# Seven block products instead of eight for two of the three input projections of a short-convolution mixer

## The reference, cut to what matters

```
h    = rms_norm(x) * gain                    # 256 x 2048
b, c, u = h @ W_in split in three            # W_in: 2048 x 6144
y    = W_out( b * causal_conv3(c * u) )      # depthwise, 3 taps, W_out: 2048 x 2048
x    = x + y
```

## Time and profile before

| | us |
|---|---|
| median of 3 runs | 2103.23 (2100.74 to 2107.02) |
| the profiled execution, device time | 2106.77 |
| its span in the trace | 2105.0 |
| PE busy | 2075.5 (99%) |
| PE weight loads busy | 1728.1 (82%) |
| VectorE busy | 1358.3 (65%) |
| ScalarE busy | 1099.4 (52%) |
| GpSimd busy | 556.6 (26%) |
| mean transfer rate | 187 GB/s |

### The profile page before, as it was taken

How to read it: one execution, slowest core, us unless ns; L and a number is a source line. 1 busy time by engine, 2 the same in 40 slices (tenths; PEclk the granted TensorE clock), 3 DMA queues, 4 the chain that set the end, 5 groups by cost and what they waited for, 6 DMA issues and landing times.

```text
span 2105.0 us, 24328 instructions
## 1 busy us (share of the span) xinstructions
PE 2075.5 (99%) x9634; PEld 1728.1 (82%) x9634; DVE 1358.3 (65%) x1378; ACT 1099.4 (52%) x1260; POOL 556.6 (26%) x292
## 2 busy tenths in 40 slices
PE   9998999999999999999999999999999999999999
PEld 8888777888888888888888888888888888888887
DVE  5787868954888358873442333478738994389832
ACT  6677555644555445554544444555545554455542
POOL 3676630023000420004454444310040003400033
PEclk9999999999999999999999999999999999999999
DMA  7533355556555565645566565556466555655554
GB/s 251 161 120 120 131 178 192 180 169 230 180 202 180 193 206 193 236 159 181 180 199 191 183 187 190 171 201 243 155 213 219 177 183 190 236 184 188 188 190 161
DMA packets 208577, 394.29 MB, mean 187 GB/s; under 512 B 11472, under 2 KB 22096, under 8 KB 208464
## 3 DMA queue, kind: packets, MB, share of 16 engines
q1 hardware_dynamic: 207888, 392.21, 55.7%
q10 hardware_dynamic: 576, 0.53, 0.1%
HBM read 390.60 MB, written 2.10 MB: 187 GB/s over the span
## 4 chain that ended last, share of the span: by engine, by line
PE 90%; issue 3%; DVE 3%; ACT 2%; POOL 1%; DMA 0%; SPq 0%; DVEq 0%; ACTq 0%; POOLq 0%
PE pair L654 14%; PE pair L656 14%; PE pair L655 14%; PE pair L731 9%; PE pair L729 9%; PE pair L730 9%; PE pair L714 5%; PE pair L715 5%; PE pair L716 5%; PE tbank L744 2%; DVE w_lo L1595 1%; DVE pair L1748 1%; POOL cv L620 1%; ACT w_hi L1161 1%; DVE s_raw L1990 0%
## 5 line engine op out<-in xcount | busy, mean ns | idle before, releaser
L1161 ACT ACTIVATE w_hi<-w_raw 128x1024 fp32r<-128x1024 f32 x608 | 642.3, 1059 | 653.5 <-PE pair L656 418.9
L608 POOL TENSOR_TENSOR w_lo<-w_raw,w_hi 128x1024 fp32r<-128x1024 f32 x191 | 472.3, 2473 | 1533.1 <-ACT w_hi L1161 1533.1
L1595 DVE TENSOR_TENSOR w_lo<-w_raw,w_hi 128x1024 fp32r<-128x1024 f32 x417 | 537.6, 1290 | 490.8 <-ACT w_hi L1161 490.6
L729 PE MATMUL pair<-w_hi,xT_hi 128*128 128x512 f32 x880 | 342.4, 389 | 0.4 <-DVE w_lo L1595 0.4
L731 PE MATMUL pair<-w_hi,xT_lo 128*128 128x512 f32 x880 | 342.4, 389 | 0.0
L730 PE MATMUL pair<-w_lo,xT_hi 128*128 128x512 f32 x880 | 342.3, 389 | 0.0
L1161 ACT ACTIVATE w_hi<-s_raw 128x1536 fp32r<-128x1536 f32 x154 | 229.2, 1488 | 160.0 <-PE pair L731 119.1
L1595 DVE TENSOR_TENSOR w_lo<-s_raw,w_hi 128x1536 fp32r<-128x1536 f32 x154 | 269.7, 1761 | 59.5 <-ACT w_hi L1161 59.2
L654 PE MATMUL pair<-w_hi,yT_hi 128*128 128x512 f32 x704 | 274.7, 390 | 0.0
L656 PE MATMUL pair<-w_hi,yT_lo 128*128 128x512 f32 x704 | 274.0, 389 | 0.0
L655 PE MATMUL pair<-w_lo,yT_hi 128*128 128x512 f32 x704 | 273.9, 389 | 0.0
(11 more groups left out here) (187 smaller groups left out, 2659.7 us busy)
## 6 DMA issues: line engine op xcount, KB each, us to landing
w_raw<-in_w_down SPq DMA_DIRECT2D x176, 512.0 KB, 4.2
w_raw<-in_w_up SPq DMA_DIRECT2D x110, 512.0 KB, 6.5
w_raw<-in_w_gate SPq DMA_DIRECT2D x110, 512.0 KB, 3.6
w_raw<-in_sc_in SPq DMA_DIRECT2D x96, 512.0 KB, 3.9
s_raw<-in_w_gate SPq DMA_DIRECT2D x44, 768.0 KB, 8.6
s_raw<-in_w_up SPq DMA_DIRECT2D x44, 768.0 KB, 8.2
w_raw<-in_w_in SPq DMA_DIRECT2D x52, 512.0 KB, 4.0
w_raw<-in_w_out SPq DMA_DIRECT2D x32, 512.0 KB, 3.5
```

What stands on the lines that cost most here:

```text
L608: nc.gpsimd.tensor_tensor(w_lo[at], raw(o), w_hi[at].bitcast(F32), ALU.subtract).then_inc(w_lo_pool, 1)
L729: nc.tensor.matmul(b, x_hi(k, t), w_hi[:, r, kk, :], start=(first[t] and kk == 0), stop=False)
L1161: nc.scalar.activation(w_hi[:, o % RING, tiles_of(o), :], raw(o), ACT.Copy).then_inc(w_hi_ready, 1)
L1595: nc.vector.tensor_tensor(w_lo[at], raw(o), w_hi[at].bitcast(F32), ALU.subtract).then_inc(w_lo_dve, 1)
```

## The change

The projections c and u (`cg` and `cu`) run as one unit `("sc", j)` of 17 slots, in the manner of the FFN's units, followed by a plain `bg` job of 8 slots, which moves to PSUM pair 1. So a block has 25 slots, and the block products leave out one of eight. Around it:

- the last `down` group of layer 0 makes the activation sums for norm 2 (`sums_first` in place of `x_split(2, 0)`, `sums_second` in place of `x_split(2, 1)`) and one more pair of operands, `xA_hi` and `xA_lo`, the plain activations of row tiles 0 to 2 and token block 1, which `bg` needs;
- its last job goes to pair 0 instead of pair 1, and VectorE adds it within the first unit;
- VectorE makes all low parts of a unit, the weight sums and the result sums; `cu`'s product is made from `snap` (`multiply_gates`);
- ACT's read-out of `bg` (`bg_out`) moves behind slot o+2 of the next unit, the gate's product and its split (`gate_products`, `gate_lows`, `z_highs`) to slots o+7 to o+9; PE's transposes of it stand behind slot o+4;
- the convolution writes into `scaled`, with token blocks outermost;
- SP loads a unit's four 768 KB blocks and ten slots in the order that the FFN's units have;
- small tables move: convolution weights of the mixer load with the first 32 KB table, others into a tensor that is freed early.

```diff
 def plan_sums(norm):
...
+        if norm == 2:
+            plan.split(("a21", norm))
...
-        plan.job(("cg", j), 0, KD)
-        plan.job(("cu", j), 1, KD)
-        plan.job(("bg", j), 2, KD)
+        plan.unit(("sc", j))
+        plan.job(("bg", j), 1, KD)
...
 # PE
+            def h_hi(k, t):
+                return xA_hi[:, k, :] if t == 1 and k < SK else x_hi(k, t)
...
+                if gate_before is not None:
+                    read_out(("bg", gate_before))
+                    block_transposes(("z", gate_before), bg_tok)
                 pe.wait_ge(pair_read[0], uses[0])
                 product(o + 5, b, xT_hi[:, 4:4 + SK, tok(0)], xT_lo[:, 4:4 + SK, tok(0)], True, False)
...
             for j in range(NJ):
                 if j:
-                    slots(("cg", j), 0, 4, x_hi, x_lo, last=SD)
-
-                    read_out(("bg", j - 1))
-                    block_transposes(("z", j - 1), bg_tok)
-                    slots(("cg", j), 4, SD, x_hi, x_lo)
-                slots(("cu", j), 0, SD, x_hi, x_lo)
-                slots(("bg", j), 0, 4, x_hi, x_lo, last=SD)
+                    unit("sc", j, gate_before=j - 1)
+                else:
+                    unit("sc", j, None, 2, ("down", 0, len(CHUNKS) - 1, NJ - 1))
+                slots(("bg", j), 0, 4, h_hi, h_lo, last=SD)
...
 # ACT
-                highs(at, o + 4)
+                highs(at, o + 3)
+                if gate_before is not None:
+                    bg_out(gate_before)
+                highs(o + 3, o + 4)
...
                 highs(o + 8, o + 9)
+                if gate_before is not None:
+                    z_highs(gate_before)
...
-                x_highs(norm_after, 0)
+                sums_highs_first(norm_after)
                 x_squares(0)
                 highs(d[2] + 5, d[2] + 8)
-                x_highs(norm_after, 1)
+                sums_highs_second(norm_after)
                 x_squares(1)
...
 # VectorE
+                if gate_before is not None:
+                    gate_products(gate_before)
                 lows(o + 8, o + 9)
+                if gate_before is not None:
+                    gate_lows(gate_before)
...
-                x_split(norm_after, 0)
+                sums_first(norm_after)
                 lows(d[2] + 5, d[2] + 8)
-                x_split(norm_after, 1)
+                sums_second(norm_after)
...
+            def multiply_gates(j):
...
+                for t in range(TT):
+                    ins = nc.vector.scalar_tensor_tensor(mixed[:, t, :], snap[:, 2 + t, :], rstd_sq[:, t:t + 1],
+                                                         snap[:, t, :], ALU.mult, ALU.mult)
...
+                s0 = JOB[("bg", j)][0]
+                lows(at, s0 + 3)
+                gate_sums("sc", j)
+                lows(s0 + 3, s0 + 4)
+                multiply_gates(j)
                 lows(s0 + 4, s0 + 7)
...
+                short_conv(j)
+                at = s0 + 7
```

More of the change, by code:

```diff
@@ L245, in encoder_kernel @@
     plan_ffn(0)
-    for b in range(NJ):
-        for t in range(TT):
-            plan.group(("x", 2, b, t), high=True, low=True)
+    plan_sums(2)
     for j in range(NJ):
-        plan.job(("cg", j), 0, KD)
-        plan.job(("cu", j), 1, KD)
-        plan.job(("bg", j), 2, KD)
+        plan.unit(("sc", j))
+        plan.job(("bg", j), 1, KD)
         for t in range(TT):
@@ L537, in ffn @@
                 ups = w_up[layer].rearrange("(k p) n -> p k n", p=P)
[L539 to L546, removed]
                 for ch, (u0, u1) in enumerate(CHUNKS):
                     for i in range(u0, u1):
[L550 to L571, removed]
+                        unit((layer, i), gates[:, :, ds(i * NB, NB)], ups[:, :, ds(i * NB, NB)])
                     k0, n = BK * u0, chunk_slots(ch)
@@ L1004, in y_transposes, with unit @@
                 block_transposes(("y", layer, i), mixed)
-            def unit(layer, i, before=None, norm=None, last_out=None):
+            def unit(layer, i, before=None, norm=None, last_out=None, gate_before=None):
                 n, o, uses = UNIT[(layer, i)]
@@ L1187, in sums_highs_first @@
                 sum_high(norm, 1, xS_hi[:, 1, :, :], sums[:, 0, 0:SK, :])
+                if norm == 2:
+                    nc.scalar.activation(xA_hi[:, :, :], raw0[:, 1, 0:SK, :], ACT.Copy).then_inc(hi_ready, 1)
             def sums_highs_second(norm):
@@ L1457, in y_highs, with bg_out, z_highs, unit @@
                     high_of_group(("y", layer, i, t), yT_hi, slice(k, k + BK), t)
-            def unit(layer, i, at, before=None, norm=None):
+            def bg_out(j):
+                s0, pair, _ = JOB[("bg", j)]
+                act.wait_ge(w_used, s0 + SD)
+                for t in range(TT):
+                    ins = nc.scalar.activation(bg_tok[:, t, :], pairs[pair][t][:, :], ACT.Copy,
+                                               scale=rstd[:, t:t + 1])
+                ins.then_inc(pair_read[pair], 1)
+            def z_highs(j):
+                for t in range(TT):
+                    high_of_scaled(("z", j, t), zT_hi, slice(BK * j, BK * (j + 1)), t)
+            def unit(layer, i, at, before=None, norm=None, gate_before=None):
                 n, o, _ = UNIT[(layer, i)]
-                highs(at, o + 4)
+                highs(at, o + 3)
+                if gate_before is not None:
+                    bg_out(gate_before)
+                highs(o + 3, o + 4)
                 if before is not None:
@@ L1516, in _ @@
             at = ffn(0, 1, at, 2)
-            def mixer_block(j):
-                s0 = JOB[("cg", j)][0]
-                if j:
-                    act.wait_ge(pair_read[1], JOB[("cu", j)][2])
-                read_pair(("cg", j), ACT.Copy, gated)
-                highs(s0 + SD + 3, s0 + 2 * SD + 7)
+            for j in range(NJ):
+                at = unit("sc", j, at, None, None if j else 2, j - 1 if j else None)
+                s0 = JOB[("bg", j)][0]
+                highs(at, s0 + 7)
                 if j:
@@ L1564, in _ @@
                 if nb == 0:
-                    for t in range(TT):
-                        high_of_scaled(("z", NJ - 1, t), zT_hi, slice(KD - BK, KD), t)
+                    z_highs(NJ - 1)
                 else:
@@ L2020, in y_lows, with unit @@
                     low_of_group(("y", layer, i, t), yT_hi, yT_lo, slice(k, k + BK), t)
-            def unit(layer, i, at, before=None, after=None, norm=None):
+            def unit(layer, i, at, before=None, after=None, norm=None, gate_before=None):
                 n, o, uses = UNIT[(layer, i)]
@@ new lines, in _ @@
+            for j in range(NJ):
+                if j:
+                    at = unit("sc", j, at, gate_before=j - 1)
+                else:
+                    at = unit("sc", j, at, None, last_down, 2)
+                s0 = JOB[("bg", j)][0]
+                lows(at, s0 + 3)
+                gate_sums("sc", j)
+                lows(s0 + 3, s0 + 4)
+                multiply_gates(j)
+                lows(s0 + 4, s0 + 7)
+                short_conv(j)
+                at = s0 + 7
+            lows(at, s0 + SD + 4)
```

195 lines of the change are left out of this document (99 added, 96 removed).

## The result

| | before | after |
|---|---|---|
| median, us | 2101.97 (2099.95 to 2107.02, 6 runs) | 2121.39 (2118.89 to 2126.80, 6 runs) |
| the profiled execution, us | 2106.77 | 2118.89 |
| its span, us | 2105.0 | 2117.0 |

The ratio is 1.0092 [1.0076, 1.0108]: the change makes the kernel 19.3 us slower, where 6.3 us less were forecast. The forecast range was 2093 to 2102 us; the result lies above it.

A forecast was written before the change was run, and what follows sets the result against it. PE was taken to bound the kernel, busy 2075.5 of 2105.0 us. Matmuls -8.16, unit 0's wait +0.52 and activation sums +1.35 gave -6.3 us, taking the median from 2103.23 to 2096.9, range 2093 to 2102.

The forecast's parts named there:

- The rest: Block loads, tables, output projection and layer 1: loads hidden by some 7 us, bigger first table under 0.1 us, others unchanged.
- The slower side of the prediction: Mixer units 1 to 3: VectorE's chain to o+9 runs 4.9 us longer than 18.2, giving 2110 us; chance 0.05.
- Rival 4: Mixer units run slower than their matmul count; called excluded by the FFN unit's 42.38 us; no size or chance given.
- Matmuls: Mixer cg and cu: 183 matmuls a unit instead of 192, 36 fewer in 4 blocks at 0.2267 us, -8.16 us.
- o+9 in unit 0: Mixer's first unit: PE waits at slot o+9 for the chain ending in bank_sum, +0.5 us, bounds 0.2 and 1.0.
- Activation sums in d2 and d3: Layer 0's last down group: the sums delay GpSimd's low for d3's first slot, PE waits, +1.35 us, bounds 0.4 to 2.1.
- Units 1 to 3: Later mixer units: bank_sum ends at T + 21.1, PE needs it by about T + 21.8, so 0 us.
- GpSimd beside the convolution: bg's last slot in blocks 0 and 2: GpSimd's low takes the port before VectorE's two-source convolution instructions, 0 us.
- The sum: Whole kernel: -8.16 + 0.52 + 1.35 = -6.3 us, median 2103.23 to 2096.9; forecast's chance 0.42.

The follow-up runs named there:

- f3: The kernel after with 96 unused bytes at the head of the late tensors, bringing xS, yT and zT back to distance 0; ratio to before 0.9970.
- n1: The kernel before with pads that move only xS, yT and zT, to distances 128, +96 and -32; ratio to before 1.0151.
- g1: The kernel before with cols ahead of xT_hi and 64 unused bytes before the late tensors, so rings and xT, xS, yT, zT shift together; ratio 0.9994.
- h1: f3 with ACT making the high part of d3's first slot before the squares of x block 1; ratio to before 0.9951.
- k1: h1 with rstd_sq behind cT, 32-word pads for 24, and three small tables in one tensor, bringing uT to distance 0; 2092.30 against 2105.32 us, ratio 0.9938.

## Why the prediction was wrong

**The step that failed** is the last part, "The rest": of the small tables that move, only the larger first transfer was priced, at less than 0.1 us, and "the output projection and layer 1 keep their parities and their one wait" was taken to mean that they keep their time. The price of 0.2267 us, read in one mixer block, was taken for every matmul of the kernel before and after. It depends on where the operands lie, and the change moved three of them. Missing in the sum: +25.2 us. The slower side of the prediction was a wait on VectorE. Rival 4, "units slower than their count", came nearest to a loss without a wait, but it was given no price and no chance, because the 42.38 us of an FFN unit were said to exclude it. They were measured in the kernel before, where `xT` and `xS` stood at distance 0, and so said nothing of a kernel in which tensors have moved.

**The steps on record, read in f3**, where the tensors are back at distance 0:

- *Matmuls, -8.16*: right. 36 fewer; the block takes 65.04 us, 65.0 were forecast.
- *o+9 in unit 0, +0.52*: right. PE's timeline of f3, 0.65 and 0.33 instead of 0.23 each, so 0.53 (a bracket is the idle time before a row and what ended it):

```profile
1050.38 0.39 PE L747 MATMUL pair<-w_hi,xT_lo 128*128 128x512 f32 x1
1051.03 0.50 PE L730 MATMUL pair<-w_hi,xS_hi 128*128 128x512 f32 x1 [0.26 <-DVE snap L1998]
1051.36 0.39 PE L731 MATMUL pair<-w_lo,xS_hi 128*128 128x512 f32 x1
```

- *Activation sums in d2 and d3, +1.35*: right in place and size, 1.18 + 0.08 = 1.26. PE's timeline of f3 at d3's first slot:

```profile
1004.48 0.39 PE L666 MATMUL pair<-w_hi,yT_lo 128*128 128x512 f32 x1
1005.89 0.47 PE L664 MATMUL pair<-w_hi,yT_hi 128*128 128x512 f32 x1 [1.02 <-POOL w_lo L618]
1006.19 0.40 PE L665 MATMUL pair<-w_lo,yT_hi 128*128 128x512 f32 x1
```

- *Units 1 to 3, 0*: right. In unit 2 of the kernel after, T is 1170.68, and VectorE's timeline has the last links of its chain:

```profile
1187.71 1.75 DVE L1595 TENSOR_TENSOR w_lo<-s_raw,w_hi 128x1536 fp32r<-128x1536 f32 x1
1189.38 1.75 DVE L1992 TENSOR_TENSOR s_raw<-s_raw 128x1536 f32<-128x1536 f32 x1
1191.05 0.68 DVE L1996 TENSOR_TENSOR snap<-pair,snap 128x512 f32<-128x512 f32 x1
```

The `bank_sum` ends at 1191.73, T + 21.05 (T + 21.1 on record). o+9 starts at T + 22.20 there, behind slower steps, and at T + 21.98 in f3 (T + 21.96 on record).

- *GpSimd beside the convolution, 0*: right, GpSimd wins, in block 0 as forecast; in block 2 it came earlier still (last section). VectorE and GpSimd in block 0 of the kernel after:

```profile
1096.15 2.48 POOL L616 TENSOR_TENSOR w_lo<-w_raw,w_hi 128x1024 fp32r<-128x1024 f32 x1 [4.42 <-ACT w_hi L1166]
```

```profile
1095.23 1.14 DVE L2177 TENSOR_SCALAR scaled<-cT,cols 128x256 f32<-128x256 f32 x4 [1.98 <-ACT cT L1554]
1096.29 5.40 DVE L2174 SCALAR_TENSOR_TENSOR scaled<-cT,cols,scaled 128x256 f32<-128x256 f32 x8
```

GpSimd takes its plain 2.48 us, and VectorE's eight instructions take 5.40 instead of 3.25. PE doesn't wait.

- *The sum, -6.3*: right. f3 against before gives -6.3 us by the ratio (between -3.4 and -9.5), and the two traces say the same.

Every term was right within 0.1 us and the forecast was 25 us off. It was not a mis-sized term but one that had no line in the working.

## What to carry to other kernels

When a change adds, drops or resizes a tensor, list the start of each matmul's stationary and moving operand before and after, and keep the difference at 0 modulo 256 bytes (shown here for fp32r with 512 columns); here 32 unused bytes were worth 17 us of 2100, more than the change itself. When busy time rises and no wait does, compare the start-to-start distance in a stretch that was not edited: a row's duration shows only 8 ns of 389, the distance over 298 steps shows it without doubt. And when an experiment adds a buffer, pin the other tensors first, or it measures the move as well.

## What the runs showed of the hardware

- The distance effect above: 226.8 ns a step at 0, 228.9 at -64, 232.4 to 234.3 at the others seen, at granted clock 1.00 in the windows shown and with weight loads of 188 ns (`yT`) in each. Behind a slow stationary tensor about ten steps of a well placed one are slower too, by 59 ns together in n1.
- GpSimd also held back VectorE's one-source instructions. In block 2 of the kernel after, GpSimd's low started at 1227.22, after the first of four convolution instructions that read `cT` alone, and these took 3.47 us where they took 1.14 in block 0. VectorE's timeline:

```profile
1226.30 3.47 DVE L2177 TENSOR_SCALAR scaled<-cT,cols 128x256 f32<-128x256 f32 x4 [2.04 <-ACT cT L1554]
1229.69 3.24 DVE L2174 SCALAR_TENSOR_TENSOR scaled<-cT,cols,scaled 128x256 f32<-128x256 f32 x8
```

The prediction had counted on their being free of it ("read one tensor only"), in an argument that changed nothing in the sum. The Trainium skill ("SBUF — State Buffer", "SBUF: two separate sides") does list `tensor_scalar` among the instructions that can take the shared pair; the 3.47 us agree.
- A stop of PE of 2 to 3 us is followed in some executions by steps of 0.43 us, the 1.2 GHz level, and in others not. After the stop at o+9 of the first FFN unit of layer 0 (1.9 to 2.1 us idle) nine of the fourteen profiled executions, those of the kernel after, f3, g1 and h1 among them, ran 7 or 8 such matmuls before 0.23 came back; in f3 the granted clock of 339.40 to 343.00 was 0.53. It costs 1.5 to 1.6 us. The execution of the kernel before ran none there, but 13 such steps after its stop of 2.9 us in front of the first product with `uT` (granted clock 0.51 from 271.30 to 277.30), and that of k1 had none at either place. This belongs to the spread of a few us between runs.
